# x and mem arrive turned from the host, parameters arrive repeated, and the first projection starts on half loads

## What is computed

```python
h = rms_norm(x, g_mix)
rq, rk, rv, rg, sq, sk, sv, mq = split(h @ w_in)           # 1024 x 2304
mk, mv = split(rms_norm(mem, g_mem) @ w_mem_kv)            # 1024 x 512
o = concat([retention(rq, rk, rv, rg), window_attention(sq, sk, sv), memory_attention(mq, mk, mv)])
x = x + o @ w_out                                          # 1024 x 1024
x = x + moe_top4_of_32(rms_norm(x, g_ffn))                 # 32 experts: w_up 1024 x 2048, w_down 1024 x 1024
```

## Time and profile before

| | us |
|---|---|
| median of three runs | 1093.05 |
| lowest and highest | 1088.51, 1093.4 |
| span of the profiled execution | 1090.2 |
| TensorE busy in it | 1000.7 (92%) |
| DVE busy | 240.1 (22%) |
| ScalarE busy | 131.4 (12%) |

### The profile page before, as it was taken

One profiled execution on the slowest core, in us unless ns is written; L12 is line 12 of the kernel. 1 busy time (PEld: TensorE's weight loads), 2 busy tenths in 40 slices (PEclk: granted clock), 3 DMA queues, 4 the chain that ended last, 5 costly groups with the idle time before them and its releaser, 6 DMA issues.

```text
span 1090.2 us, 11471 instructions
## 1 busy us (share of the span) xinstructions
PE 1000.7 (92%) x4559; PEld 412.2 (38%) x4559; DVE 240.1 (22%) x553; ACT 131.4 (12%) x241; POOL 12.3 (1%) x24
## 2 busy tenths in 40 slices
PE   8999999999999898899889898998889998989897
PEld 5446553443434232242424242433324242424233
DVE  2237242130303030211212030302112120303021
ACT  4117120101000000010100000000101000000000
POOL 0200000000000000000000000000000000000000
PEclk9999989999999999999999999999999999999999
DMA  9853859999999999999999999999999999999995
GB/s 344 305 205 130 320 204 393 368 412 421 419 421 419 422 421 419 422 419 423 419 422 419 423 419 423 421 420 421 420 421 421 421 421 421 419 422 421 420 422 207
DMA packets 67977, 422.74 MB, mean 388 GB/s; under 512 B 4925, under 2 KB 6358, under 8 KB 22902
## 3 DMA queue, kind: packets, MB, share of 16 engines
q1 hardware_dynamic: 67536, 422.06, 94.4%
q10 hardware_dynamic: 422, 0.41, 0.1%
HBM read 421.41 MB, written 1.05 MB: 388 GB/s over the span
## 4 chain that ended last, share of the span: by engine, by line
PE 43%; SPq 28%; DMA 24%; issue 2%; DVE 1%; ACT 1%; ACTq 0%
SPq L415 18%; PE psum L1321 13%; DMA ring<-in_w_up 12%; DMA work<-in_w_up 12%; PE psum L1365 11%; SPq L420 6%; PE psum L1051 4%; PE psum L1244 4%; SPq L426 4%; PE psum L1177 3%; PE psum L1006 2%; PE psum L1274 2%; PE psum L1043 1%; PE psum L1033 1%; PE psum L1234 0%
## 5 line engine op out<-in xcount | busy, mean ns | idle before, releaser
L1321 PE MATMUL psum<-ring,work 128*64 128x512 f32 x1520 | 352.1, 609 | 51.6 <-DMA ring<-in_w_up 50.7
L1321 PEld LDWEIGHTS psum<-ring,work 128*64 128x64 f32 x1520 | 106.5, 139 | 290.9 <-issue 208.1
L1365 PE MATMUL psum<-ring,work 128*64 128x512 f32 x752 | 165.1, 594 | 5.0 <-ACT work L655 2.8
L1321 PE MATMUL psum<-work 128*64 128x512 f32 x528 | 119.6, 597 | 18.8 <-DMA work<-in_w_up 18.8
L944 DVE TENSOR_TENSOR xy<-psum,xy 128x512 f32<-128x512 f32 x68 | 47.0, 692 | 233.7 <-PE psum L1274 233.7
L1365 PEld LDWEIGHTS psum<-ring,work 128*64 128x64 f32 x752 | 57.8, 137 | 101.0 <-issue 101.0
L648 ACT ACTIVATE work<-work 128x512 f32<-128x512 f32 x32 | 20.2, 630 | 577.3 <-DVE work L974 577.3
L893 DVE TENSOR_SCALAR work<-const 128x128 f32<-128x128 f32 x17 | 4.7, 279 | 362.1 <-PE psum L1234 362.1
L1321 PEld LDWEIGHTS psum<-work 128*64 128x64 f32 x528 | 35.4, 136 | 102.1 <-issue 62.5
L1274 PE MATMUL psum<-work 128*128 128x512 f32 x136 | 68.8, 631 | 2.2 <-issue 2.2
L1244 PE MATMUL psum<-work 128*128 128x128 f32 x544 | 65.0, 278 | 0.0
(11 more groups left out here) (169 smaller groups left out, 420.4 us busy)
## 6 DMA issues: line engine op xcount, KB each, us to landing
ring<-in_w_up SPq DMA_DIRECT2D x95, 2048.0 KB, 28.5
ring<-in_w_down SPq DMA_DIRECT2D x39, 2048.0 KB, 32.7
work<-in_w_up SPq DMA_DIRECT2D x32, 2048.0 KB, 28.3
work<-in_w_down SPq DMA_DIRECT2D x9, 2048.0 KB, 32.6
ring<-in_w_down SPq DMA_DIRECT2D x16, 1024.0 KB, 29.1
work<-in_w_down SPq DMA_DIRECT2D x16, 1024.0 KB, 28.9
ring<-in_w_in SPq DMA_DIRECT2D x4, 2048.0 KB, 19.8
ring<-in_w_out SPq DMA_DIRECT2D x2, 2048.0 KB, 10.0
```

The costliest lines, as they stand in the source:

```text
L1321: mm = pe.matmul(psum[r:r + SLOTS, n], XT[:, j, r:r + SLOTS], weights[e][:, n * N:(n + 1) * N], start=i == 0 and not first, stop=last, ski ...
L1365: mm = pe.matmul(psum[r:r + SLOTS, 4 + n], actT[:, 2 * i + k, r:r + SLOTS], weights[e][:, k * D + n * N:k * D + (n + 1) * N], start=i == 0 ...
```

## The change

The host hands over x and mem twice: row-wise as before, and turned, as [128, 8, 256] arrays. The turned ones are loaded straight into hT and memT, and the gains are multiplied in place, on DVE for x (8 instructions of 128x256 in place of four of 128x512 from PSUM), on ScalarE for mem (8 as before, from SBUF in place of PSUM). The gains come as [128, 24] and the small parameters as [128, 292], repeated by the host. TensorE's turns of x, mem and gains, and the product that spread the parameters, are gone, and so are DVE's two copies of them. SP's order is now: first half of turned x, first half of w_mq, second halves of both, x, constants, turned mem, mem, w_mem, and the rest as before. The first tile of the mq projection runs k = 0 to 3 when the first half of w_mq has landed and waits for the second ahead of k = 4. The waits on the constants and on ones move to their first users.

```diff
 # SP
+            half = KD // 2
+            for i, done in ((0, w_mq_in), (1, landed[2])):
+                sp.dma_start(hT[:, i * half:(i + 1) * half], x_turned[:, i * half:(i + 1) * half]).then_inc(xT_in[i], 16)
+                sp.dma_start(w_mq_sb[:, i * half:(i + 1) * half],
+                             w_in[0, i * half * P:(i + 1) * half * P, 2048:2304].rearrange("(k p) n -> p k n", p=P)
+                             ).then_inc(done, 16)
+            for t in range(TILES):
+                sp.dma_start(xy[:, t], x[0, t * P:(t + 1) * P, :]).then_inc(x_in[t], 16)
             sp.dma_start(const[:, 0:CONST_FIRST], constants[:, 0:CONST_FIRST]).then_inc(const_in, 16)
-            for t in range(TILES):
-                sp.dma_start(xy[:, t], x[0, t * P:(t + 1) * P, :]).then_inc(x_in[t], 16)
-            sp.dma_start(w_mq_sb, w_in[0, :, 2048:2304].rearrange("(k p) n -> p k n", p=P)).then_inc(landed[2], 16)
+            sp.dma_start(memT, mem_turned).then_inc(memT_in, 16)
             for t in range(TILES):
                 sp.dma_start(mem_sb[:, t], mem[0, t * P:(t + 1) * P, :]).then_inc(mem_in[t], 16)
             sp.dma_start(w_mem_sb, w_mem_kv[0].rearrange("(k p) n -> p k n", p=P)).then_inc(landed[0], 16)
 # ScalarE
-            act.dma_start(norm_rows, norm_gains).then_inc(params_in, 16)
-            act.dma_start(param_row, small_params).then_inc(params_in, 16)
+            act.dma_start(norm_gain[:], norm_gains).then_inc(gains_in, 16)
             act.dma_start(pos_i[:], positions).then_inc(pos_in, 16)
+            act.dma_start(param[:], small_params).then_inc(params_in, 16)
...
-            act.wait_ge(params_ready, 2)
+            act.wait_ge(gains_in, 16)
+            act.wait_ge(memT_in, 16)
             for k in range(KD):
-                if k % 2 == 0:
-                    act.wait_ge(mem_turned, k // 2 + 1)
-                nc.scalar.activation(memT[:, k], psum[:, MEMT_BANKS[k // 2], (k % 2) * 256:(k % 2 + 1) * 256], ACT.Copy,
-                                     scale=norm_gain[:, KD + k:KD + k + 1]).then_inc(memT_ready, 1)
+                nc.scalar.activation(memT[:, k], memT[:, k], ACT.Copy, scale=norm_gain[:, KD + k:KD + k + 1]
+                                     ).then_inc(memT_ready, 1)
+            act.wait_ge(params_in, 16)
 # DVE
-            dve.wait_ge(params_spread, 2)
-            V.tensor_copy(norm_gain[:], psum[:, 7, 0:3 * KD]).then_inc(params_ready, 1)
-            V.tensor_copy(param[:], psum[:, 7, 64:64 + ROW_COLS]).then_inc(params_ready, 1)
...
-            for i in range(4):
-                dve.wait_ge(x_turned, i + 1)
-                turned_gain(hT[:, 2 * i:2 * i + 2], psum[:, 3 + i], 0, 2 * i, 2, 256).then_inc(hT_ready, 1)
+            dve.wait_ge(gains_in, 16)
+            for k in range(KD):
+                if k % (KD // 2) == 0:
+                    dve.wait_ge(xT_in[k // (KD // 2)], 16)
+                V.tensor_scalar(hT[:, k], hT[:, k], norm_gain[:, k:k + 1], None, ALU.mult).then_inc(hT_ready, 1)
             dve.wait_ge(pos_in, 16)
+            dve.wait_ge(const_in, 16)
...
+            dve.wait_ge(params_in, 16)
             V.tensor_copy(swa_gain[:, 0:4], parameter("swa_q").unsqueeze(1).to_broadcast([P, 4, DH]))
 # TensorE
-            turn(psum[:, 7, 0:3 * KD], norm_rows).then_inc(params_spread, 1)
-            pe.matmul(psum[:, 7, 64:64 + ROW_COLS], ones[0:1, :], param_row, start=True, stop=True
-                      ).then_inc(params_spread, 1)
...
-            turn_rows(xy, (3, 4, 5, 6), x_in, x_turned)
-            pe.wait_ge(params_ready, 2)
-            pe.wait_ge(landed[2], 16)
+            pe.wait_ge(w_mq_in, 16)
             for t in range(TILES):
                 for k in range(KD):
-                    if t == 0 and k % 2 == 0:
-                        pe.wait_ge(hT_ready, k // 2 + 1)
+                    if t == 0:
+                        if k == KD // 2:
+                            pe.wait_ge(landed[2], 16)
+                        pe.wait_ge(hT_ready, k + 1)
...
-            turn_rows(mem_sb, MEMT_BANKS, mem_in, mem_turned)
...
+            pe.wait_ge(const_in, 16)
             pe.wait_ge(mk_ready, 2)
 # host
+def turned_rows(x):
+    n, d = x.shape
+    return x.reshape(n, d // P, P).transpose(2, 1, 0)
...
+        "norm_gains": np.concatenate(gains, 0).T,
+        "small_params": np.broadcast_to(np.concatenate(params, 1), (P, ROW_COLS)),
```

More of the change, by code:

```diff
@@ L102, in shape_constants, with layer_kernel @@
     return c
-def layer_kernel(nc, x, mem, positions, norm_gains, w_in, w_mem_kv, small_params, w_out, w_router, w_up, b_up,
+def layer_kernel(nc, x, mem, x_turned, mem_turned, positions, norm_gains, w_in, w_mem_kv, small_params, w_out, w_router, w_up, b_up,
                  w_down, b_down, constants, out):
@@ L120, in layer_kernel @@
     MQ_BANKS = RV_BANKS = RET_O_BANKS = (2, 7)
-    MEMT_BANKS = MIXED_BANKS = (0, 1, 3, 4)
+    MIXED_BANKS = (0, 1, 3, 4)
     HEAD_BANKS = (5, 6, 0, 1)
@@ L203, in layer_kernel @@
         start_cols = rg.rearrange("p t n -> p (t n)")
-        norm_rows = start_cols[0:3 * KD, 0:P]
-        param_row = start_cols[0:1, P:P + ROW_COLS]
         turns = start_cols[:, 512:512 + 2 * TILES * (DH // 2)].rearrange("p (a t n) -> p a t n", a=2, t=TILES)
@@ L295, in layer_kernel @@
             sem("const_in"), sem("tables_in"), [sem("x_in0"), sem("x_in1")], [sem("mem_in0"), sem("mem_in1")])
-        pos_in, params_in, router_in = sem("pos_in"), sem("params_in"), sem("router_in")
+        pos_in, gains_in, params_in, router_in = sem("pos_in"), sem("gains_in"), sem("params_in"), sem("router_in")
+        xT_in, memT_in, w_mq_in = [sem("xT_in0"), sem("xT_in1")], sem("memT_in"), sem("w_mq_in")
         bup_in, bdown_in, out_written = sem("bup_in"), sem("bdown_in"), sem("out_written")
@@ L305, in layer_kernel @@
         rstd = {n: sem(f"rstd_{n}") for n in ("mem", "x", "mk", "mq", "swa", "ret", "ffn")}
-        params_spread, params_ready = sem("params_spread"), sem("params_ready")
         angles_ready, trig_ready, decay_ready = sem("angles_ready"), sem("trig_ready"), sem("decay_ready")
         rotation_ready = sem("rotation_ready")
-        mem_turned, memT_ready = sem("mem_turned"), sem("memT_ready")
-        x_turned, hT_ready = sem("x_turned"), sem("hT_ready")
+        memT_ready, hT_ready = sem("memT_ready"), sem("hT_ready")
         mkv_done, mv_ready, mk_ready = sem("mkv_done"), sem("mv_ready"), sem("mk_ready")
@@ L392, in _ @@
         def _(sp):
-            sp.dma_start(const[:, 0:CONST_FIRST], constants[:, 0:CONST_FIRST]).then_inc(const_in, 16)
+            half = KD // 2
[4 more added lines that the diff above has]
+                             ).then_inc(done, 16)
             for t in range(TILES):
                 sp.dma_start(xy[:, t], x[0, t * P:(t + 1) * P, :]).then_inc(x_in[t], 16)
-            sp.dma_start(w_mq_sb, w_in[0, :, 2048:2304].rearrange("(k p) n -> p k n", p=P)).then_inc(landed[2], 16)
+            sp.dma_start(const[:, 0:CONST_FIRST], constants[:, 0:CONST_FIRST]).then_inc(const_in, 16)
+            sp.dma_start(memT, mem_turned).then_inc(memT_in, 16)
             for t in range(TILES):
@@ L688, in turned_gain @@
                 return V.tensor_tensor(dst, src.rearrange("p (k n) -> p k n", k=kn), g, ALU.mult)
-            dve.wait_ge(params_ready, 2)
-            for i in range(4):
-                dve.wait_ge(x_turned, i + 1)
-                turned_gain(hT[:, 2 * i:2 * i + 2], psum[:, 3 + i], 0, 2 * i, 2, 256).then_inc(hT_ready, 1)
+            dve.wait_ge(gains_in, 16)
[3 more added lines that the diff above has]
+                V.tensor_scalar(hT[:, k], hT[:, k], norm_gain[:, k:k + 1], None, ALU.mult).then_inc(hT_ready, 1)
             dve.wait_ge(pos_in, 16)
+            dve.wait_ge(const_in, 16)
             step(V.tensor_copy(posf, pos_i[:]))
@@ L1006, in turn @@
                 return pe.transpose(dst, src, ident[0:n, 0:n])
-            pe.wait_ge(const_in, 16)
-            pe.wait_ge(ones_ready, 1)
-            pe.wait_ge(params_in, 32)
-            turn(psum[:, 7, 0:3 * KD], norm_rows).then_inc(params_spread, 1)
-            pe.matmul(psum[:, 7, 64:64 + ROW_COLS], ones[0:1, :], param_row, start=True, stop=True
-                      ).then_inc(params_spread, 1)
-            def turn_rows(src, banks, arrived, done):
-                for t in range(TILES):
[L1018 to L1023, removed]
-            turn_rows(xy, (3, 4, 5, 6), x_in, x_turned)
-            pe.wait_ge(params_ready, 2)
-            pe.wait_ge(landed[2], 16)
+            pe.wait_ge(w_mq_in, 16)
             for t in range(TILES):
                 for k in range(KD):
-                    if t == 0 and k % 2 == 0:
-                        pe.wait_ge(hT_ready, k // 2 + 1)
+                    if t == 0:
+                        if k == KD // 2:
+                            pe.wait_ge(landed[2], 16)
+                        pe.wait_ge(hT_ready, k + 1)
```

(7 more changed lines are left out.)

## The result

| | median us | ratio to before, 95% interval |
|---|---|---|
| before (6 runs beside it) | 1091.62 (1088.51 to 1093.4) | |
| changed kernel (6 runs) | 1096.47 (1094.7 to 1097.02) | 1.0051 [1.0037, 1.0065] |

The change costs 0.51%, 5.6 us of 1091.6 by the ratio, 4.85 us between the medians (1096.47 - 1091.62). The forecast was +4.9 us. The profiled execution took 1096.26 us with a span of 1094.4, so 1.9 us lie around the span.

A forecast was written before the change was run, and what follows sets the result against it. The DMA stream of expert weights bounds the kernel, its start set by TensorE's front. Late w_mem +3.2 us and half clock +1.7 make +4.9: 1093.05 + 4.9 = 1098.0 us, range 1092.8 to 1101.0.

The forecast's parts named there:

- The point to watch and the bound: Memory projection's start is the point; expert weights stream at DMA rate, and a front shift reaches the end one to one.
- rival E: Slack between 85 and 200 us swallows the shift, or the router stage's half clock differs; 1093 to 1095 us, chance 0.12.
- w_mem at 24.0 us: Added 2194 KB delay w_mem's landing from 18.35 us by 5.3 to 5.8, so the memory projection starts 3.2 us later.
- First projection: mq projection: 4 of 32 matmuls run on first halves, the rest from 10.3 us, ending likely near 18.5 us.
- The half loads give nothing back: At the mq projection: it ends before 24.0 us either way, then TensorE stands and waits for w_mem.
- The clock: TensorE idles about 18.5 to 24.0 us, then runs the memory projection partly at half clock: +1.7 us, bounds 0 and 3.4.
- Rival B: Ahead of the memory projection: late w_mem but clock kept, +2.9 to +3.4 us, 1096.2 us; chance 0.20.
- the dense row near 603 us: Earlier trace: after a 2.25 us transfer wait, 16 matmuls took 5.38 us instead of 3.65; taken as the 1.7 us loss.
- Rival C: From the memory projection on: a long half-clock spell, +3.2 + 3.4 = 6.6 us, 1099.6 us; chance 0.20.
- The rest at nothing: DVE products, ScalarE squares and gains, tables and waits on constants in the front are hidden by transfers or other work.
- Rival D: w_mem lands by the end of mq, so is no bound; 0.2 to 2.3 us gained, 1090.8 to 1092.9 us; chance 0.06.
- A: The forecast itself: late w_mem and one half-clock spell at the memory projection, 1098.0 us (1096.8 to 1099.0); chance 0.42.

The follow-up runs named there:

- best: Changed kernel with x_turned whole, w_mq in halves, then turned mem, w_mem in halves, and x, constants and mem behind them; ratio 0.9961, median 1085.42 us.
- wmem_halves2: As wmem_early2, with w_mem too in two halves, the memory projection's first tile starting on the first; ratio 0.9964, -3.9 us.
- early_whole: As wmem_early2, with x_turned and w_mq loaded whole instead of in halves; ratio 0.9980, -2.2 us.
- wmem_early2: Changed kernel with turned mem and w_mem issued right behind w_mq, ahead of x, constants and mem, gains of memT ahead of squares; ratio 0.9994, -0.7 us.
- warm8: Changed kernel with 8 unused 128x512 products on TensorE between the mq projection and the wait for w_mem; ratio 1.0034, +3.7 us.
- bytes2: Kernel before with 2048 KB of extra loads (x and mem once more) issued ahead of mem and w_mem, all turns kept; ratio 1.0025, +2.7 us.
- whole: Changed kernel with x_turned and w_mq loaded whole instead of in halves; ratio 1.0036, +3.9 us.
- warm16: Changed kernel with 16 unused 128x512 products on TensorE between the mq projection and the wait for w_mem; ratio 1.0093, +10.1 us.
- half_x: Changed kernel with only x_turned in halves, w_mq whole between them; single time 1095.34 us.
- half_w: Changed kernel with only w_mq in halves, x_turned whole; single time 1095.36 us.
- param_late: Changed kernel with the repeated small parameters issued on ScalarE's queue behind the squares of x and mem; single time 1096.31 us.
- packed: Changed kernel with the two halves of x_turned laid out one behind the other by the host, each 512 KB in one piece; single time 1093.48 us.

## Why the prediction was right, step by step

**The point to watch and the bound.** Right. The time follows one number of the front, the start of the w_in projections in the chain of waits. The runs that have an interval:

| kernel | w_in projections start, us | against before | time against before, us (ratio x 1090.6) |
|---|---|---|---|
| best | 30.77 | -4.0 | -4.3 |
| wmem_halves2 | 30.93 | -3.9 | -3.9 |
| early_whole | 31.90 | -2.9 | -2.2 |
| wmem_early2 | 33.15 | -1.6 | -0.7 |
| before | 34.79 | | |
| warm8 | 38.45 | +3.7 | +3.7 |
| bytes2 | 38.51 | +3.7 | +2.7 |
| whole | 39.25 | +4.5 | +3.9 |
| changed kernel | 40.28 | +5.5 | +5.6 |
| warm16 | 44.51 | +9.7 | +10.1 |

Over 14 us of front the time follows within 1 us, inside the intervals, which reach 1.3 to 2 us to each side. The pass-through is shown; rival E's slack that swallows the shift is out. A single execution shows it less well: in all fourteen traces the last pair's gather (L1229 in the changed kernel) begins 1024.5 to 1028.2 us behind the start of the w_in projections. So the four single times scatter: half_x begins them at 41.33 us (+6.5), half_w at 38.68 (+3.9), and took 1095.34 and 1095.36 us; param_late has +5.5 and took 4.6 us more than the run beside it, packed +4.7 and 2.8. The other half of rival E, a later stage that meets its half clock otherwise, is seen in the profiled execution (+1.0 and -1.69 us above), not in the medians.

**w_mem at 24.0 us.** It landed at 24.35. The size came out right by luck; its parts were wrong. The bytes cost less than I said: 2194 KB with whole loads put w_mem from 18.35 to 22.6 us, 4.3 us, and bytes2 paid 4.4 us for 2048 KB, where I had 5.3 to 5.8 at 387 to 421 GB/s. And the strided halves of x_turned cost 1.7 us that I had at nothing. The two errors all but cancelled. Why the added rows seem to go by faster than the stage's own rate, the windows up to the landing tell in part; bytes are rate times length. Before, 323 GB/s over 18.35 us are 5.93 MB; in whole, 348 over 22.63 are 7.88; in bytes2, 343 over 22.82 are 7.83. So 1.95 and 1.90 MB more had moved, not the 2.25 and 2.10 that were added: fewer bytes of the transfers behind w_mem went by ahead of its landing. And the rate rose, in whole to 377 GB/s from 296 between 3 and 6 us, in bytes2 to 413 from 389 between 10 and 14; why it did in the second, where the DMA share was near 1 in both, is open. The prediction's sum took the bytes ahead of w_mem as all that moves, at one rate.

**First projection.** I had it end near 18.5 us; it ended at 16.69. Two readings were off. I counted the records of the profile (x32) as products, so that "only 4 of the 32" could start on the first halves; the program has 16 products for mq, of two records each, and a quarter of them could. And the second half of w_mq landed at 2.19 + 8.9 = 11.1 us, not by 10.6. The count is the smaller part of the miss: 28 records from 11.1 us at the prediction's fast 0.218 us would have ended at 17.2; up to 18.5 it was the guess at how long the slow start lasts. None of it changed the sum, since the end of mq isn't what the memory projection waits for; it did set the gap, 7.70 us and not 5.5. "The half loads give nothing back" stands for this order of transfers, and understates: they cost. In the order of the best run, half loads of w_mq and w_mem work.

**The clock.** +1.7 forecast, +1.92 in the trace, 1.9 by warm8, which had the same start without the gap. Rival B (clock kept) is out for this kernel. That the dense row near 603 us gave the right size was luck within a range, as the seven traces with a longer wait ahead of the memory projection show:

| kernel | wait, us | memory projection, us | over 13.97 |
|---|---|---|---|
| wmem_early2 | 1.75 | 14.00 | 0.0 |
| bytes2 | 2.44 | 15.70 | 1.7 |
| whole | 3.75 | 16.57 | 2.6 |
| half_w | 5.22 | 16.02 | 2.1 |
| half_x | 5.68 | 16.95 | 3.0 |
| packed | 6.79 | 16.91 | 2.9 |
| param_late | 7.63 | 15.98 | 2.0 |
| changed kernel | 7.70 | 15.89 | 1.9 |

The cost doesn't grow with the wait. What sets it within 1.7 to 3.0 us is open, one trace each. Rival C (3.4 us) didn't come in the changed kernel, but half_x and packed come near it.

**The rest at nothing.** The gains, the squares, the tables and the waits on constants were all hidden, as said. Rival D, by which w_mem would be no bound, fell with the landing. It asked for the right thing in the wrong way: w_mem can be there by the end of mq, not by a faster transfer but by an earlier place in the queue.

**The chances.** Slower by over 0.5% had 0.42, within 0.5% 0.54; the ratio of 1.0051 lies on that border, its interval on both sides. The measured 1096.47 is 1.5 us under the forecast of 1098.0, most of it because the prediction started from a median of 1093.05 and the kernel before came out at 1091.62 with six runs. By the time alone it would have been rival B (1096.2); it is the trace that says A.

## What to carry to other kernels

A step that is moved off an engine onto the DMA queue pays with the bytes that it puts ahead of the next transfer that anyone waits for. Write down the landing of that transfer and its first use; here the margin was 2.5 us and the bytes took 4.3. Then order the queue by first use, and put half loads where the engine waits. Look at how a half lies in memory: x_turned in pieces of 4 KB out of every 8 cost 1.7 us here, while w_mq, which is 1 KB out of each row of 9 KB whole or halved, cost nothing by being halved (half_w against whole, w_mem at 22.6 us in both). A gap costs more than its length: waits of 2.44 to 7.70 us cost TensorE another 1.7 to 3.0 us at half clock behind them.

## What the runs showed of the hardware that was not expected

- The first transfers of the kernel, as pieces of 4 KB out of every 8, ran at 214 GB/s between 3 and 6 us; the same bytes packed ran at 347, and whole at 377.
- A gap of TensorE of 1.75 us (wmem_early2) left the clock at full and one of 2.44 us (bytes2) did not, in front of the same matmuls. They aren't quite the same case: ahead of the first stood the mq projection, ahead of the second 1.9 us of turns. In the earlier trace rows, both times behind down projections, 2.17 us left it at full and 2.25 us did not.
- Behind gaps of 2.44 to 7.70 us the same 32 records took 1.7 to 3.0 us longer, and not the most behind the longest.
- In the projections an f32 product of 128x128 by 128x512 is two records of the profile, 0.43 us each at full clock.
